# Down products of an encoder trunk: weight sums moved from the down stage to the z stage and kept in memory, gate sums moved to VectorE

## What is computed

```python
z = rmsnorm(x, norm_g) @ w_in                    # 1024 x 2312, feeds three mixers
x = x + mixed @ w_out
up = rmsnorm(x, ffn_norm) @ w_up                 # 1024 x 5632
c = conv_b + sum(full[:, j:j + T] * conv_w[j])   # causal, width 3
y = (gelu(c[..., :2816]) * c[..., 2816:]) @ w_down   # 2816 x 1024
x = x + y
```

## Time and profile before

| | |
|---|---|
| time, median of 3 runs (range) | 2413.76 us (2410.37 to 2416.2) |
| the profiled execution: time, span | 2414.81 us, 2413.0 us |
| PE busy, PEld busy | 2360.4 us (98%), 2315.0 us (96%) |
| DVE, ACT, POOL busy | 1682.6 (70%), 1116.8 (46%), 742.7 us (31%) |
| moved by DMA | 264.83 MB, mean 110 GB/s |

### The profile page before, as it was taken

One profiled execution on the slowest core, in us unless ns is written; L12 is line 12 of the kernel. 1 busy time (PEld: TensorE's weight loads), 2 busy tenths in 40 slices (PEclk: granted clock), 3 DMA queues, 4 the chain that ended last, 5 costly groups with the idle time before them and its releaser, 6 DMA issues.

```text
span 2413.0 us, 42532 instructions
## 1 busy us (share of the span) xinstructions
PE 2360.4 (98%) x16563; PEld 2315.0 (96%) x16563; DVE 1682.6 (70%) x2875; ACT 1116.8 (46%) x2227; POOL 742.7 (31%) x732
## 2 busy tenths in 40 slices
PE   9999999999999999999999999999999999998999
PEld 8999998999999998999999999999999999998999
DVE  3115687888788877888611256877987888779884
ACT  6325676544433433345523366655333333333563
POOL 0001254432222223664110013452322222245630
PEclk9999999999999999999999999999999999999999
DMA  4442432212221224454524334321222222253564
GB/s 155 135 142 89 147 114 53 73 64 81 72 80 64 81 72 150 161 165 137 196 73 139 120 125 136 100 60 54 81 78 74 72 73 75 86 214 93 161 198 148
DMA packets 248348, 264.83 MB, mean 110 GB/s; under 512 B 16822, under 2 KB 212564, under 8 KB 245972
## 3 DMA queue, kind: packets, MB, share of 16 engines
q1 hardware_dynamic: 248148, 262.11, 34.3%
HBM read 211.95 MB, written 50.11 MB: 109 GB/s over the span
## 4 chain that ended last, share of the span: by engine, by line
PE 78%; DVE 12%; issue 4%; POOL 2%; ACT 2%; DMA 2%; SPq 0%; DVEq 0%; POOLq 0%; ACTq 0%
PE bank L401 24%; PE bank L403 23%; PE bank L402 23%; DVE sA L2729 3%; DVE sB L2731 3%; PE bank L1367 1%; PE bank L1292 1%; PE bank L1337 1%; DMA grr<-g_scratch 1%; DVE xT L2740 1%; DVE tb L2726 1%; PE bank L1377 1%; POOL wN L2187 1%; POOL acc L453 1%; DVE sD L2731 1%
## 5 line engine op out<-in xcount | busy, mean ns | idle before, releaser
L401 PE MATMUL bank<-actH,wb 128*128 128x384 f32 (+1 forms) x1712 | 560.8, 328 | 1.5 <-DVE actL L2607 1.3
L402 PE MATMUL bank<-actL,wb 128*128 128x384 f32 (+1 forms) x1712 | 555.5, 324 | 0.0
L403 PE MATMUL bank<-actH,wb 128*128 128x384 f32 (+1 forms) x1712 | 555.1, 324 | 0.0
L401 PE MATMUL bank<-wzH,actH 128*128 128x256 f32 (+3 forms) x1296 | 369.4, 285 | 2.8 <-issue 1.5
L403 PE MATMUL bank<-wzH,actL 128*128 128x256 f32 (+3 forms) x1296 | 364.2, 281 | 0.0
L402 PE MATMUL bank<-wzL,actH 128*128 128x256 f32 (+3 forms) x1296 | 363.9, 281 | 0.0
L401 PEld LDWEIGHTS bank<-actH,wb 128*128 128x128 f32 x1712 | 322.8, 189 | 6.2 <-issue 3.2
L402 PEld LDWEIGHTS bank<-actL,wb 128*128 128x128 f32 x1712 | 323.7, 189 | 0.7
L403 PEld LDWEIGHTS bank<-actH,wb 128*128 128x128 f32 x1712 | 323.7, 189 | 0.0
L401 PEld LDWEIGHTS bank<-wzH,actH 128*128 128x128 f32 (+1 forms) x1296 | 236.3, 182 | 4.9 <-issue 2.0
L402 PEld LDWEIGHTS bank<-wzL,actH 128*128 128x128 f32 (+1 forms) x1296 | 236.5, 182 | 0.0
(11 more groups left out here) (361 smaller groups left out, 5526.6 us busy)
## 6 DMA issues: line engine op xcount, KB each, us to landing
raw<-in_w_up SPq DMA_DIRECT2D x88, 512.0 KB, 4.5
g_scratch<-cv SPq DMA_DIRECT2D x44, 545.0 KB, 3.1
rawz<-in_w_in SPq DMA_DIRECT2D x22, 1024.0 KB, 5.4
zb<-z_scratch SPq DMA_DIRECT2D x16, 1156.0 KB, 6.1
z_scratch<-zst SPq DMA_DIRECT2D x128, 128.0 KB, 1.8
raw<-in_w_out SPq DMA_DIRECT2D x128, 128.0 KB, 2.9
grr<-g_scratch SPq DMA_DIRECT2D x38, 384.0 KB, 3.3
raw<-in_w_down SPq DMA_DIRECT2D x50, 256.0 KB, 3.4
```

Of the source, the lines that this page charges most:

```text
L401: pe.matmul(out, aH, bH, start=first, stop=False, skip_group_check=goes_on)
L402: pe.matmul(out, aH, bL, start=False, stop=False, skip_group_check=goes_on)
L403: return pe.matmul(out, aL, bH, start=False, stop=last, skip_group_check=goes_on)
```

## The change

- A step t = NJ*p + j replaces the units for everything but PE: one load, one ACT copy and one DVE subtraction for both halves h of the weights (128x2x512), and one each for both halves of the gates (128x2x384). In p = 3 a step has one half. There are 44 steps a layer and four slots (`sA0`, `sA1`, `sA3`; `sB`, `sB3`); a slot is free when both units of step t-4 are done. PE's units and their order stay; each waits for its step.
- The weight sums are made in the z stage on POOL (`weight_parts`, four 128x512 instructions for each j) from 1 MB of `w_down` that SP loads at u = 9, 12, ..., 39 (`load_parts`) into two places `stg`, and are stored as 1 MB at u = 13, 16, ..., 43 (`store_sums`) to `ws_scratch` in memory. `load_parts(i)` waits for the store of i-2. `stg` lies where `zb` lies later, so `load_zb(0)` waits for the last two stores. POOL makes six of the eleven before it clears the mixers' tiles.
- In the down stage `load_w` reads the sums from memory. A step of p = 0, 1, 2, 3 loads 512, 512, 512, 256 KB of weights and 384, 192, 576, 192 KB of gate pieces (before: 768, 256, 256, 0 and 384, 192, 576, 192). All four gate sums are DVE's (`gate_sum`), made one step ahead, the sum in place in `pbA`, `pbB` or `grr`. `load_w` waits for the parts of t-4, and `load_gs` in p = 2 for those of t-3.
- POOL keeps only the sums of squares in the down stage.
- The two transposes of the convolution state move from after unit (0, 0, 0) to after unit (3, 1, 2), into bank 2.
- On DVE both halves' additions to `xT` stand after step j = 1 of the next p.
- In the last layer the first four splits of the plain part wait for later units (`half_high`: 7, 7, 9, 10 in place of 1).

The core of the diff:

```diff
+        ws_dram = nc.dram_tensor("ws_scratch", (DEPTH, NJ, P, 4, 512), F32, kind="Internal").ap()
...
+        def g_pair(j):
+
+            return pbA[:, j] if j < 6 else pbB[:, j - 6]
...
+        def slot_free(l, t):
+
+            if t < 4:
+                return tile_mm(l, NF - 1, (2, 6, 9, 9)[t])
+            p, j = (t - 4) // NJ, (t - 4) % NJ
+            if t >= 3 * NJ:
+                return unit_mm(l, p, 1, j)
+            return max(unit_mm(l, p, h, j) for h in range(2))
...
+                    elif i == 0:
+                        sp.wait_ge(ws_st[0], ws_stored(l, NJ - 1))
+                        sp.wait_ge(ws_st[1], ws_stored(l, NJ - 2))
...
+                def load_parts(i):
+                    if i >= 2:
+                        sp.wait_ge(ws_st[i % 2], ws_stored(l, i - 2))
+                    sp.dma_start(stg[:, i % 2, 0:4].rearrange("p (k h) n -> p k (h n)", k=2),
+                                 w_down[2 * i * P:2 * i * P + 2 * P, :].rearrange("(k p) n -> p k n", p=P)).then_inc(ws_in[i % 2], 16)
+
+                def store_sums(i):
+                    sp.wait_ge(s_r, w_sum_at(l, i, 3))
+                    sp.dma_start(ws_dram[l, i], stg[:, i % 2, 1:5]).then_inc(ws_st[i % 2], 16)
+
                 for u in range(Z1):
                     store_z(u)
+                    if u >= 9 and u % 3 == 0 and u // 3 - 3 < NJ:
+                        load_parts(u // 3 - 3)
+                    if u >= 13 and u % 3 == 1 and u // 3 - 4 < NJ:
+                        store_sums(u // 3 - 4)
...
+                    if t >= 4:
+                        sp.wait_ge(w_l, step_low(l, t - 4))
+                    place, r0, r1 = w_raw(t), slice(2 * j * P, 2 * j * P + P), slice(2 * j * P + P, 2 * j * P + 2 * P)
                     if p == 0:
-                        sp.dma_start(w_raw(f), w_down[f * P:f * P + P, :]).then_inc(ld_in[t % 3], 16)
-                    c = slice(0, 512) if p == 1 else slice(512, 1024)
-                    sp.dma_start(w_raw(f + 1)[:, c], w_down[f * P + P:f * P + 2 * P, c]).then_inc(ld_in[t % 3], 16)
+                        sp.dma_start(place[:, 0], ws_dram[l, j, :, 3]).then_inc(ld_in[t % 3], 16)
+                        sp.dma_start(place[:, 1], w_down[r0, 0:512]).then_inc(ld_in[t % 3], 16)
+                    elif p == 1:
+                        sp.dma_start(place[:, 0:2], ws_dram[l, j, :, 1:3]).then_inc(ld_in[t % 3], 16)
+                    elif p == 2:
+                        sp.dma_start(place[:, 0], w_down[r1, 0:512]).then_inc(ld_in[t % 3], 16)
+                        sp.dma_start(place[:, 1], ws_dram[l, j, :, 0]).then_inc(ld_in[t % 3], 16)
+                    else:
+                        sp.dma_start(place[:, 1], w_down[r1, 512:1024]).then_inc(ld_in[t % 3], 16)
...
+                    if p in (1, 3):
+                        sp.wait_ge(w_l, step_low(l, t - NJ if p == 1 else t - 2 * NJ))
+                    elif p == 2 and j >= 3:
+                        sp.wait_ge(w_l, step_low(l, t - 3))
...
-                for t in range(2, 5):
+                for t in range(3, 4 * NJ):
                     load_w(t)
-                for t in range(4, 4 * NJ):
                     load_gs(t)
-                    if t + 1 < 3 * NJ:
-                        load_w(t + 1)
-                    if t == 7:
+                    if t == 9:
...
+                    pe.wait_ge(w_l, step_low(l, t))
...
-                    if (p, h, j) == (0, 0, 0):
+                    if (p, h, j) == (3, 1, 2):
                         pe.wait_ge(cvs_r, (l + 1) * 4 * NF)
+                        pe.wait_ge(bank_free, product_out(l, 2, 0, 2))
...
+                def step_high(t):
+
+                    raw_w, w_hi, _ = w_parts(t)
+                    raw_g, g_hi, _ = g_parts(t)
+                    act.wait_ge(mm, slot_free(l, t))
+                    act.wait_ge(ld_in[t % 3], ld_at(l, t))
+                    act.activation(w_hi, raw_w, ACT.Copy).then_inc(w_h, 1)
+                    act.wait_ge(s_l, g_sum_at(l, t))
+                    act.activation(g_hi, raw_g, ACT.Copy).then_inc(w_h, 1)
...
-                        unit_high(0, 0, 1)
-                        unit_high(0, 1, 0)
-                        unit_high(0, 1, 1)
+                        step_high(1)
+                        step_high(2)
+                        step_high(3)
                     gelu(p)
-                unit_high(0, 0, 2)
                 conv_first(NF - 1, 1)
 
-                act.wait_ge(stt_r, 2 * l + 2)
-                act.wait_ge(gv_st, l * 16 + 16)
-                act.activation(cvo, bank[7][0:88, 0:256].rearrange("p (s t) -> p s t", s=2), ACT.Copy).then_inc(sto_r, 1)
...
+                def weight_parts(i):
+
+                    A11, A21, A12, A22, S1 = (stg[:, i % 2, k] for k in range(5))
+                    pool.wait_ge(ws_in[i % 2], ws_loaded(l, i))
+                    pool.tensor_tensor(S1, A21, A22, ALU.add).then_inc(s_r, 1)
+                    pool.tensor_tensor(A21, A11, A21, ALU.subtract).then_inc(s_r, 1)
+                    pool.wait_ge(s_r, w_sum_at(l, i, 0))
+                    pool.tensor_tensor(A22, S1, A11, ALU.subtract).then_inc(s_r, 1)
+                    pool.wait_ge(s_r, w_sum_at(l, i, 2))
+                    pool.tensor_tensor(A12, A12, A22, ALU.subtract).then_inc(s_r, 1)
+
+                for i in range(6):
+                    weight_parts(i)
...
+                for i in range(6, NJ):
+                    weight_parts(i)
...
-                def unit_sums(p, h, j):
-
-                    t = NJ * p + j
-                    A11, A12, A21, A22 = (w_block(j, m, k) for m in range(2) for k in range(2))
-                    raws = g_raws(p, j)
-                    if (p, h) == (0, 0):
-                        pool.wait_ge(ld_in[t % 3], ld_at(l, t))
-                        pool.tensor_tensor(A22, A21, A22, ALU.add).then_inc(s_r, 1)
...
-                for p, h, j in UNITS:
-                    unit_sums(p, h, j)
-                    if (p, h) == (2, 0) and 5 <= j < 8:
+                for t in range(4 * NJ):
...
-                def unit_low_parts(p, h, j):
-
-                    t = NJ * p + j
-                    a, g = w_slot(p, h, j), g_slot(p, h, j)
-                    if (p, h) == (1, 1):
-                        dve.wait_ge(ld_in[t % 3], ld_at(l, t))
-                        dve.tensor_tensor(tb[:, j], g_raws(p, j)[:, 0], tb[:, j], ALU.subtract).then_inc(s_l, 1)
-                    count = unit_low(l, p, h, j)
-                    dve.wait_ge(w_h, count - 1)
-                    dve.tensor_tensor(a[:, 1], w_source(p, h, j), a[:, 0].bitcast(F32), ALU.subtract).then_inc(w_l, 1)
-                    dve.wait_ge(w_h, count)
-                    dve.tensor_tensor(g[:, 1], g_source(p, h, j), g[:, 0].bitcast(F32), ALU.subtract).then_inc(w_l, 1)
+                def gate_sum(t):
+
+                    p, j = t // NJ, t % NJ
+                    first, second = g_pair(j)[:, 0], g_pair(j)[:, 1]
+                    dve.wait_ge(ld_in[t % 3], ld_at(l, t))
+                    if p in (1, 3):
+                        dve.wait_ge(w_l, step_low(l, j if p == 1 else NJ + j))
+                    out, x, y = ((first, first, second), (first, second, first), (grr[:, j % 3, 2], grr[:, j % 3, 0], grr[:, j % 3, 2]),
+                                 (second, second, first))[p]
+                    dve.tensor_tensor(out, x, y, ALU.subtract).then_inc(s_l, 1)
+
+                def step_parts(t):
+
+                    if t + 1 < 4 * NJ:
+                        gate_sum(t + 1)
+                    raw_w, w_hi, w_lo = w_parts(t)
+                    raw_g, g_hi, g_lo = g_parts(t)
+                    dve.wait_ge(w_h, step_low(l, t) - 1)
+                    dve.tensor_tensor(w_lo, raw_w, w_hi.bitcast(F32), ALU.subtract).then_inc(w_l, 1)
+                    dve.wait_ge(w_h, step_low(l, t))
+                    dve.tensor_tensor(g_lo, raw_g, g_hi.bitcast(F32), ALU.subtract).then_inc(w_l, 1)
...
-                        unit_low_parts(0, 1, 0)
-                        unit_low_parts(0, 1, 1)
-                        unit_low_parts(0, 0, 2)
+                        step_parts(2)
                     tap(p, 1, 1)
                     if p == NF - 1:
-                        unit_low_parts(0, 1, 2)
+                        step_parts(3)
                     tap(p, 1, 2)
                     if p == NF - 1:
-                        unit_low_parts(0, 0, 3)
+                        step_parts(4)
...
-                        unit_low_parts(0, 0, 0)
+                        gate_sum(0)
+                        step_parts(0)
                     tap(p, 0, 1)
                     dve.wait_ge(take_r, take_at(l, p, 5))
                     take(p, 8, upb2[:, U0], 3, upb2[:, U0])
+                    if not ahead:
+                        step_parts(1)
                     tap(p, 0, 2)
                     if ahead:
                         sum_low(p + 1, 3)
-                    else:
```

(39 more changed lines are left out.)

235 lines of the change are left out of this document (77 added, 158 removed).

## The result

The changed kernel takes 2422.3 us (median of 9 runs, 2417.3 to 2424.2) against 2414.4 for the kernel before (9 runs, 2410.4 to 2418.5): ratio 1.0030, 95% interval 1.0022 to 1.0039. I had predicted 2380.0 (2368 to 2403), so **the prediction was wrong**: outside its range and of the other sign. The profiled execution has a span of 2420.5 us.

The account below looks back on a forecast made before the run. PE, 98% busy, was taken to bound the kernel, waiting mainly for DVE in the down stage. -48.6 + 4 (loads) + 4 (start) + 6 (z stage) = -34.6 us from 2414.8 gave 2380 us, range 2368 to 2403.

Parts of the forecast that it names:

- Term 1: Steady down stage: PE's waits for xT and parts go, -48.6 us for both layers, with 4 us back for loads.
- B: Down stage: landings of its loads set the pace in p = 2 and 3; 2390 us, or 2405; chance 0.12.
- D: Down stage: POOL did not cause DVE's long instructions, so PE's waits stay; no gain, 2414 to 2420 us; chance 0.04.
- Term 2: Start of the down stage: gate sums and wider parts delay PE's first units, +4 us for two layers.
- Term 3: z stage: added loads, stores and sums delay PE at group 5, 3 us a layer, +6 for both (bounds 0 and 40).
- the ring of the sums: z stage: a round's load, sums and store with two places take 8.0 or 9.7 us, against 8.5 for three tiles.
- the one group that POOL's clearing makes tight: z stage, w_in group 5: 5.8 us to spare before; each us of later landing would cost PE one.
- bandwidth sum: z stage: at 410 GB/s the added 23.1 MB take 56 us, with 40 us of present use 96 of 97 us.
- Rival A: z stage: DMA engines full at 360 GB/s, 7 us a layer above the time; 2388 us, or 2394; chance 0.14.
- Rival C: z stage: the ring of sums in SP's queue sets the pace, slower than before from 8.5 us landings; chance 0.08.

Follow-up runs that it names:

- e1: Changed kernel with only its down stage: no block fetched, summed or stored in the z stage, unsummed w_down blocks read instead; 2367.6 us, ratio 0.9808.
- e4: Changed kernel with full-size sums, but after the first two rounds of a layer each round fetches and stores only 16 columns; 2367.6 us.
- e5: Changed kernel with the w_in group issued ahead of a round's fetch or store after the same z tile; 2416.2 us.
- e7: Changed kernel with the rounds' fetches issued from ScalarE's queue instead of SP's, after the same z tiles; 2416.0 us.
- e6: Changed kernel with a layer's eleven rounds spread over 41 z tiles instead of 34, behind the w_in group of the same tile; 2403.0 us, ratio 0.9960.
- e13: Changed kernel with 1.5 MB a round instead of 2, rounds placed by w_in groups, ACT's high parts one evacuation later except the last group's; 2375.7 us, ratio 0.9838.
- e3: Changed kernel without the stores of the sums, fetch and sums at full size, down stage reading unsummed w_down blocks; 2379.0 us.
- e14: Changed kernel with its full 2 MB a round, but rounds placed by w_in groups and ACT's high parts later except the last group's; 2389.5 us, ratio 0.9898.

## Why the prediction was wrong, point by point

- **Term 1** held. The down stage reached 162.7 us against the 161.4 at pace that I had computed plus 2 for loads. The gain is 45.9 where I had 44.6. Rivals B and D fell with it: DVE's parts have the lengths I gave (`sB` 0.952 at the median against my 0.95 in proportion, `sA` 1.22), with few long ones (1.78 at most), and PE's waits in the stage are 0.3 us.
- **Term 2** was small: in e1 the first unit starts at 943.9, 1.0 us later than before; I had 2 a layer.
- **Term 3 failed: "I take 3 us a layer", with "Later groups had 9 us to spare".** It measured 23.9 us in layer 0 and 30.9 in layer 1, against e1. I followed the ring of the sums, at landings of 5.4 and 7.1 us, and the one group that POOL's clearing makes tight, where I priced the clearing; e4, with the clearing and all sums in place, loses nothing. I left the landing of the `w_in` groups themselves at what it was. It nearly doubled, 5.4 to 9.9 us, for groups that share one raw place. Every group has to pass that ring, so the 9 us were not slack to be used once: in a ring of 14.1 us that needed 5.4 + 1.9 + 2.3 = 9.6, the 4.5 us more of landing use up all that is left, and each us that SP's order adds before the issue is passed on to the next group. For the last group the 9 us were not there at all: it had 0.3 us to spare in the kernel before (149.58 to 149.90), and it took the longest stall of each layer, 11.2 and 12.7 us.
- **The bandwidth sum** was made with the wrong yardstick. The reading behind it, that most slices of the busy stretch show 390 to 429 GB/s, is wrong: 13 of the 29 slices at 125 GB/s or more do, and these 29 average 338. It asked whether 96 of 97 us suffice, and had I believed 360 GB/s it would have given 7 us a layer. Slices of 95:150 do reach 451 GB/s in the change, but others there fall to 32, and the stretch means 311 (after), 317 (e5), 328 (e7). That the waits in the ring leave these gaps is my reading of it. At 311 the sum would have been 74 + 40 = 114 us of 97, an estimate of 17 us a layer. The Trainium skill, DMA: Bandwidth & Descriptors, section Specifications, gives about 358 GB/s a core; slices above it, seen here on a chip with one core at work, show that it is no ceiling in this case, yet it would have been the better planning figure.
- **Rival A** came nearest to the mechanism, and I gave its sign ("`w_in` groups landing after 8 us or more"), at 14 us for both layers, a quarter of its price. I priced the missing bandwidth alone, not the ring, ACT's order or the clock. PE's z waits sum to 43.4 us against 1.9 in e1; of 54.7 that leaves some 13 us for the slow clock after them. PE's busy time, in which the slow stretches count, says the same: 2356.3 us against 2342.3 for the same 16563 matmuls.
- **Rival C** had the price (slower from 20.3 us a layer) with the wrong mechanism. SP waited for POOL 3.5 us in 95:180, at most 1.5 at a time. The other wait of its ring, for the landing of a store, was longer (14.4 us, at most 3.8), and it stands ahead of groups of `w_in`. But in 95:180 e6 is without it and still loses 35 us, e7 (where ACT waits in SP's place) 48, and e13 has as much of it (14.3 us) and loses 8; what share it has in the change no run shows.

## What to carry to other kernels

Before traffic is put under a stage whose engines it does not touch, list the transfers that already feed the stage, and for each the ring it closes (issue, landing, use, free place) and that ring's slack. Price the new traffic by what it does to these landings, not by whether total bytes fit. Put bulk transfers behind the urgent ones and not within two tiles ahead, cut the bytes that another stage with idle engines can make itself, and take an in-order engine's wait for a load as late as its deadline allows.

## What the runs showed of the hardware

Landing time under load was the surprise. With 2 MB of rounds in 8.5 us of z products, a 1 MB group of `w_in` landed after 9.9 us at the median of 95:150 (5.4 in the kernel before), and a store of 128 KB after 5.8 (1.9 before); with 1 MB of rounds (e3) they were 6.0 and 4.1. Stores of 1 MB took longer than fetches of 1 MB where SP issued both, 7.9 against 6.1 in the change and 8.7 against 6.1 in e14; with the fetches on ScalarE's queue (e7) it turned round, 6.2 against 7.3. And one stall is paid twice: after a wait of 11.2 us the granted clock was 0.61 in the window of 10 us in which it ended.
